# A merge and an output projection whose first inputs are loaded one stage earlier, and a last tile of a layer norm that another engine scales

## The reference, cut to what matters

```python
z = x @ w_in + b_in        # its last 3072 columns are mg, the pre-activations of three merge gates
# branch A: causal conv, RG-LRU scan, gelu gate        -> ya (1024 wide)
# branch B: stick-breaking attention                   -> yb (512 wide)
# branch C: mLSTM matrix memory in blocks, layer norm  -> yc (512 wide), and the new states c, n, m
mix = sigmoid(g_a) * (ya @ w_pa) + sigmoid(g_b) * (yb @ w_pb) + sigmoid(g_c) * (yc @ w_pc)
x1  = LN1(alpha * x + mix @ w_out)
y   = LN2(alpha * x1 + MoE(x1) + sigmoid(x1 @ Wg + bg) * (p @ Wp))     # top 4 of 32 experts
```

## Time and profile before

| | us |
|---|---|
| median of 3 runs | 2816.36 (2815.64 to 2816.7) |
| the profiled execution, its own time | 2818.67 |
| its span, first to last instruction | 2816.9 |
| TensorE busy in the span | 2557.3 (91%) |
| VectorE busy | 1580.7 (56%) |
| ScalarE busy | 1332.0 (47%) |
| GpSimd busy | 622.9 (22%) |
| merge, first to last matmul | 944.2 to 1445.4 |
| output projection, first matmul to end of the stage | 1452.4 to 1577.3 |

### The profile page before, as it was taken

The page is one execution under the profiler, slowest core; times in us unless marked ns, Lnnn a source line. Parts: engine busy times, 40 slices in busy tenths (PEclk is TensorE's granted clock), DMA queues, the critical chain, the costliest instruction groups (busy, mean ns, idle before and its releaser), DMA issues. The chain is left out here.

```text
span 2816.9 us, 40711 instructions
## 1 busy us (share of the span) xinstructions
PE 2557.3 (91%) x15168; PEld 2299.0 (82%) x15168; DVE 1580.7 (56%) x2533; ACT 1332.0 (47%) x2070; POOL 622.9 (22%) x494
## 2 busy tenths in 40 slices
PE   7998799999888799999989888599999999999990
PEld 6997687887567699999978567599999999998990
DVE  4665312118557545445444465577777777777774
ACT  4665311116432443334331222477777777777762
POOL 1000100004101011010114231143343343333433
PEclk9999989999999799999999899799999999999995
DMA  8221223202482755565543311688888898898864
GB/s 250 73 61 43 71 79 114 86 27 105 170 271 63 153 150 144 129 157 142 136 140 114 104 53 64 220 276 256 264 273 246 274 273 247 272 270 251 272 190 160
DMA packets 391375, 467.99 MB, mean 166 GB/s; under 512 B 21565, under 2 KB 314549, under 8 KB 391258
## 3 DMA queue, kind: packets, MB, share of 16 engines
q1 hardware_dynamic: 369160, 395.81, 45.9%
q0 software_dynamic: 17760, 60.34, 8.9%
q10 hardware_dynamic: 4338, 10.23, 0.9%
HBM read 397.62 MB, written 68.70 MB: 166 GB/s over the span
## 5 line engine op out<-in xcount | busy, mean ns | idle before, releaser
L3120 PE MATMUL banks<-slot_rowsT,expert_w_high 128*128 128x384 f32 x2048 | 603.7, 363 | 0.2 <-DVE slot_rowsT L3221 0.2
L3122 PE MATMUL banks<-slot_rowsT,expert_w_low 128*128 128x192 f32 x2048 | 515.2, 252 | 0.0
L3122 PEld LDWEIGHTS banks<-slot_rowsT,expert_w_low 128*128 128x128 f32 x2048 | 392.6, 192 | 1.3
L3120 PEld LDWEIGHTS banks<-slot_rowsT,expert_w_high 128*128 128x128 f32 x2048 | 385.8, 188 | 2.0 <-issue 0.6
L3156 ACT CAST expert_w_high<-expert_w 128x2048 fp32r<-128x2048 f32 x128 | 238.1, 1909 | 20.5 <-DMA expert_w<-in_exp_w 20.5
L3215 DVE TENSOR_TENSOR expert_w_low<-expert_w,expert_w_high 128x2048 fp32r<-128x2048 f32 x96 | 216.8, 2285 | 21.0 <-ACT expert_w_high L3156 21.0
L2068 PE MATMUL banks<-xT_chunk_high,w_gates_high 128*128 128x384 f32 x576 | 193.3, 336 | 15.7 <-DVE xT_chunk_low L2136 15.7
L3025 POOL TENSOR_TENSOR expert_w_low<-expert_w,expert_w_high 128x2048 fp32r<-128x2048 f32 x32 | 147.7, 4616 | 266.8 <-ACT expert_w_high L3156 266.8
L2069 PE MATMUL banks<-xT_chunk_low,w_gates_high 128*128 128x384 f32 x576 | 193.1, 335 | 0.0
L2070 PE MATMUL banks<-xT_chunk_high,w_gates_low 128*128 128x384 f32 x576 | 193.0, 335 | 0.0
L3281 DVE TENSOR_TENSOR expert_w_low<-expert_w,expert_w_high 128x1024 fp32r<-128x1024 f32 x128 | 157.2, 1228 | 54.5 <-ACT expert_w_high L3185 54.5
(11 more groups left out here) (498 smaller groups left out, 6122.8 us busy)
## 6 DMA issues: line engine op xcount, KB each, us to landing
expert_w<-in_exp_w SPq DMA_DIRECT2D x128, 1024.0 KB
expert_w<-in_exp_w SPq DMA_DIRECT2D x32, 2048.0 KB
w_gates<-in_w_in SPq DMA_DIRECT2D x72, 512.0 KB, 4.6
cached_k<-in_cache_sb_k SPq DMA_DIRECT2D x16, 1024.0 KB, 10.3
cached_v<-in_cache_sb_v SPq DMA_DIRECT2D x16, 1024.0 KB, 11.1
w_stream<-in_w_in SPq DMA_DIRECT2D x48, 256.0 KB, 4.4
w_proj<-in_w_pa SPq DMA_DIRECT2D x24, 512.0 KB, 5.1
w_stream<-in_w_in SPq DMA_DIRECT2D x16, 512.0 KB, 5.0
```

Source lines behind the costliest of these rows:

```text
L3120: nc.tensor.matmul(out[:, 0:2 * SLOTS], hi, xgT[:, par, k].rearrange("p a s -> p (a s)"), start=(k == 0), stop=(k == DT - 1), skip_group_c ...
L3122: last = nc.tensor.matmul(out[:, 0:SLOTS], lo, xgT[:, par, k, 0, :], start=False, stop=(k == DT - 1), skip_group_check=True)
```

## The change

- A new class `MixInputs` owns the merge's raw tiles `xa`, `wg`, `wp` and their DMA semaphores. It is made before `stage_mlstm`, and its `load_ahead` is called in that stage's SyncE stream behind `m.o_gate`: gate weights of unit 0, both halves of x's first chunk, projection weights of unit 0, then both weights of unit 1. `stage_mix` loads only from unit 2 on.
- In the merge, the casts and low parts of unit 0 stand in another order: gate weights, x, projection weights.
- A new class `OutInputs` owns the ring of `w_out` pieces and its semaphores. The ring has three places and not four. Its first three pieces are loaded at the end of the merge's SyncE stream; `stage_out` loads the other 13.
- The multiply and the add of the first norm's last row tile stand on VectorE behind its normalise, and no longer on GpSimd; those who read the tile wait for a new semaphore, `x1_last`.
- The new semaphores live in a second `stage_semaphores` of `early`, so there is one more clearing and barrier where `early` closes, between the routing and the experts.

```diff
@@ stage_mlstm, SyncE
             sp.dma_start(m.o_gate[:], g.mo_d.rearrange("i p n -> p i n")).then_inc(o_in, 16)
+            load_ahead(sp)
             sp.wait_ge(c_ready, 8)
@@ MixInputs
+    def load_ahead(self, sp):
+        self.load_gate_w(sp, 0, 1, 0)
+        self.load_x(sp, 0)
+        self.load_proj_w(sp, 0, 1, 0)
+        self.load_gate_w(sp, 1, 1, 1)
+        self.load_proj_w(sp, 1, 1, 1)
@@ OutInputs
+    WR = 3
+    def load(self, sp, n):
+        half, k = divmod(n, DT)
+        sp.dma_start(self.w[:, n % self.WR, :], self.source[:, k, half * 512:(half + 1) * 512]
+                     ).then_inc(self.w_in[n % self.WR], 16)
@@ stage_mix, SyncE (end)
+            for n in range(OutInputs.WR):
+                out_early.load(sp, n)
@@ stage_mix, ScalarE (VectorE the same with the low parts)
-            w_high_part(0)
+            gate_w_high_part(0)
             x_high_part(0)
+            proj_w_high_part(0)
@@ stage_out
-    R, WR = 3, 4
+    R, WR = 3, OutInputs.WR
@@ stage_out, SyncE
-            for n, (half, k) in enumerate(pieces):
-                if n >= WR:
-
-                    sp.wait_ge(w_split, n - WR + 1)
-                sp.dma_start(w[:, n % WR, :], wv[:, k, half * 512:(half + 1) * 512]).then_inc(w_in[n % WR], 16)
+            for n in range(WR, len(pieces)):
+
+                sp.wait_ge(w_split, n - WR + 1)
+                early.load(sp, n)
@@ stage_out, VectorE (end)
+            dve.wait_ge(norm_in, 32)
+            dve.wait_ge(hat_ready, NT)
+            nc.vector.tensor_tensor(x[:, s, :], x[:, s, :], norm[:, 0, :], ALU.mult).then_inc(last_scaled, 1)
+            dve.wait_ge(last_scaled, 1)
+            nc.vector.tensor_tensor(x[:, s, :], x[:, s, :], norm[:, 1, :], ALU.add).then_inc(x1_last, 1)
@@ stage_out, GpSimd
-            for i in range(NT):
+            for i in range(NT - 1):
@@ build_program
+                sem = early.enter_context(stage_semaphores(nc))
+                mix_early = MixInputs(nc, late, sem, g)
...
+                with ExitStack() as pieces:
+                    out_early = OutInputs(nc, pieces, sem, g)
+                    stage_mix(nc, g, xT, qT, ycT, mix_early, out_early)
+                    late.close()
+                    sem = early.enter_context(stage_semaphores(nc))
+                    route = RouteInputs(nc, early, sem, g)
+                    stage_out(nc, g, xT, xT, out_early, route.load_ahead)
```

More of the change, by code:

```diff
@@ L1972, in _, with __init__, sb, load_gate_w @@
                 nc.vector.tensor_tensor(hc[:, i, :], hc[:, i, :], m.o_gate[:, i, :], ALU.mult).then_inc(yc_ready, 1)
-def stage_mix(nc, g, mixT, yb, yc):
+class MixInputs:
+    def __init__(self, nc, ctx, sem, g):
+        def sb(name, shape):
+            return ctx.enter_context(nc.sbuf_tensor(name, shape, F32))
+        self.g = g
+        self.xa = sb("xT_then_yaT_chunk", [P, DT, CHUNK3])
+        self.wg, self.wp = sb("w_gates", [P, 2, DT, P]), sb("w_proj", [P, 2, DT, P])
+        self.x_in = [sem("x_x_in0"), sem("x_x_in1")]
+        self.wg_in = [sem(f"x_wg_in{i}") for i in range(2)]
+        self.wp_in = [sem(f"x_wp_in{i}") for i in range(2)]
+        self.src = ((g.w_pa, DT, 0), (g.w_pb, H, 0), (g.w_pc, H, H))
+    def load_gate_w(self, sp, n, r, m):
+        col = O_MG + r * D + m * P
+        sp.dma_start(self.wg[:, n % 2], self.g.w_in[0].rearrange("(k p) n -> p k n", p=P)[:, :, col:col + P]
+                     ).then_inc(self.wg_in[n % 2], 16)
+    def load_proj_w(self, sp, n, r, m):
+        w, kn, _ = self.src[r]
+        sp.dma_start(self.wp[:, n % 2, 0:kn, :], w[0].rearrange("(k p) n -> p k n", p=P)[:, :, m * P:(m + 1) * P]
+                     ).then_inc(self.wp_in[n % 2], 16)
+    def load_x(self, sp, c):
+        for half in range(2):
+            k = slice(4 * half, 4 * half + 4)
+            sp.dma_start(self.xa[:, k, :],
+                         self.g.xT_d.rearrange("k p t -> p k t")[:, k, c * CHUNK3:(c + 1) * CHUNK3]
+                         ).then_inc(self.x_in[half], 16)
+    def load_ahead(self, sp):
[4 more added lines that the diff above has]
+        self.load_proj_w(sp, 1, 1, 1)
+class OutInputs:
+    WR = 3
+    def __init__(self, nc, ctx, sem, g):
+        self.w = ctx.enter_context(nc.sbuf_tensor("w_out_piece", [P, self.WR, 512], F32, side="right"))
+        self.w_in = [sem(f"o_w_in{i}") for i in range(self.WR)]
+        self.source = g.w_out[0].rearrange("(k p) n -> p k n", p=P)
+    def load(self, sp, n):
+        half, k = divmod(n, DT)
+        sp.dma_start(self.w[:, n % self.WR, :], self.source[:, k, half * 512:(half + 1) * 512]
+                     ).then_inc(self.w_in[n % self.WR], 16)
+def stage_mix(nc, g, mixT, yb, yc, early, out_early):
     ORDER = [(r, m) for r in (1, 2, 0) for m in range(DT)]
@@ L1989, in stage_mix @@
         y_lo = sb("yT_chunk_low", [P, 2 * H, CHUNK3], F32R)
[L1990 to L1991 removed]
+        xa, wg, wp, x_in, wg_in, wp_in = early.xa, early.wg, early.wp, early.x_in, early.wg_in, early.wp_in
         wg_hi = sb("w_gates_high", [P, 2, DT, P], F32R)
         wg_lo = sb("w_gates_low", [P, 2, DT, P], F32R)
[L1994 removed]
         wp_hi = sb("w_proj_high", [P, 2, DT, P], F32R)
@@ L2015, in stage_mix @@
         block = ctx.enter_context(nc.Block())
-        SRC = ((g.w_pa, DT, 0), (g.w_pb, H, 0), (g.w_pc, H, H))
+        SRC = early.src
         Y_PARTS = {0: (0, yb, 0), 1: (H, yc, 0), DT: (0, xa, 0), 2 * DT: (H, xa, H)}
@@ L2024, in _ @@
         def _(sp):
[L2025 to L2031, removed]
             for n, (c, r, m) in enumerate(units):
@@ L2036, in _ @@
                     sp.wait_ge(wg_split, n - 1)
[L2037 to L2041, removed]
+                    early.load_gate_w(sp, n, r, m)
                     sp.wait_ge(wp_split, n - 1)
-                w, kn, _ = SRC[r]
-                sp.dma_start(wp[:, n % 2, 0:kn, :], w[0].rearrange("(k p) n -> p k n", p=P)[:, :, m * P:(m + 1) * P]
-                             ).then_inc(wp_in[n % 2], 16)
+                    early.load_proj_w(sp, n, r, m)
                 if n % U == 2 * DT + 2 and c + 1 < C:
                     sp.wait_ge(y_split, 4 * H * (c + 1))
-                    load_x(c + 1)
+                    early.load_x(sp, c + 1)
                 if n % U == 3:
@@ L2181, in _, with stage_out @@
                                        ALU.add).then_inc(add_ready, 1)
-def stage_out(nc, g, mixT, x1T, load_ahead):
-    R, WR = 3, 4
+def stage_out(nc, g, mixT, x1T, early, load_ahead):
+    R, WR = 3, OutInputs.WR
+    w, w_in = early.w, early.w_in
     pieces = [(half, k) for half in range(2) for k in range(DT)]
@@ L2202, in stage_out @@
         mv = sb("ln1_mean_var", [P, R, 2])
-        w_in = [sem(f"o_w_in{i}") for i in range(WR)]
         w_high = sem("o_w_high")
@@ L2251, in turn @@
             def turn(i):
-                pe.wait_ge(x1_ready, i + 1)
+                if i < NT - 1:
+                    pe.wait_ge(x1_ready, i + 1)
+                else:
+                    pe.wait_ge(x1_last, 1)
                 for half in range(2):
@@ L3471, in build_program @@
                     m.v_aug, m.o_gate = rb("ml_v", [P, NT, H, HD + 1]), rb("ml_o", [P, NT, 512])
-                    stage_mlstm(nc, g, m, ycT)
+                    stage_mlstm(nc, g, m, ycT, mix_early.load_ahead)
                 xT = early.enter_context(nc.sbuf_tensor("xT", [P, DT, T], F32, side="right"))
[L3474 to L3478, removed]
+                with ExitStack() as pieces:
[5 more added lines that the diff above has]
+                    stage_out(nc, g, xT, xT, out_early, route.load_ahead)
                 stage_route(nc, g, xT, route)
```

33 lines of the change are left out of this document (19 added, 14 removed).

## The result

| | before | changed |
|---|---|---|
| median, 15 runs each, us | 2814.46 (2809.12 to 2819.21) | 2804.51 (2798.04 to 2811.33) |
| ratio | | 0.9964, 95% interval 0.9955 to 0.9973 |
| the profiled execution, its own time | 2818.67 | 2800.07 |

The kernel became faster by 0.36%, 10.1 us of 2814.46 (7.6 to 12.7 by the interval). I had forecast a gain of 7.0 and a time of 2809.4, between 2806.3 and 2813.4. The sign and the order of size are right.

What follows compares the result with a forecast made beforehand. The prediction took TensorE's waits at stage starts and ends, with barriers that absorb nothing, to bound the kernel. Terms 9.0 - 3.8 + 2.3 - 0.5 = 7.0 us gave 2816.36 - 7.0 = 2809.4, range 2806.3 to 2813.4.

Steps and rivals of the forecast that it cites:

- What bounds the kernel, and where: Whole kernel: gains lie where TensorE stands still; stages end in barriers, so a shorter stage moves everything behind it.
- Part 1: Merge start: inputs loaded ahead let the first matmul start 9.0 us earlier, bounds 8.0 to 9.3.
- Part 2: Output projection, w_out ring of three: five rounds with landing time 3.2 us lose 3.8 us, bounds 1.3 to 6.8.
- The rival in which the ring is as fast as a lone load: Output projection's w_out ring: landing time 2.7, loss only 1.3 us, total gain 9.5, time 2806.9; chance 0.19.
- Part 3: End of output projection: last tile's two passes on VectorE instead of GpSimd gain 2.3 us, bounds 2.0 to 2.4.
- Part 4: Ahead of the experts: one more clearing and barrier costs 0.5 us, bounds 0.4 to 0.7.
- The clock: Rival: ring gaps put the second row tile at half clock, 2.0 us lost, 2811.4; chance 0.29, including landing above 3.6.
- The sum: Whole kernel: 9.0 - 3.8 + 2.3 - 0.5 = 7.0 us gained.
- The time: Whole kernel: median 2816.36 less 7.0 gives 2809.4 us, range 2806.3 to 2813.4.
- The chance of faster: Whole kernel: 0.64 that the measurement tells it faster, against same 0.33 and slower 0.03.

Runs made afterwards that it cites:

- again: The changed kernel profiled a second time with no edit; merge 507.7 us, output projection 128.3 us.
- e3: Changed kernel with the last tile's multiply and add back on GpSimd; output projection 130.6 us, merge 506.7 us.
- e4: Changed kernel with the old order of casts and low parts of unit 0 (gate weights, projection weights, x); merge 508.2 us.
- e6: Changed kernel with a second ring of eight places for the other 13 w_out pieces; median 2797.7 us, ratio 0.9934 to the kernel before.
- e2: Kernel before with a ring of three and not four w_out pieces, nothing loaded ahead; output projection 133.5 us, last low part 25.5 us behind the barrier.
- e5: Changed kernel with two places for w_out pieces, both loaded during the merge; output projection 137.9 us, last low part 33.0 us behind the barrier.

## Why the prediction was wrong, step by step

**What bounds the kernel, and where.** Right, as far as the scatter lets it be seen. The stages add up: nothing behind a barrier absorbed a gain or repaid one by more than the scatter of the later stages.

**Part 1, 9.0 us.** Right. The start of the merge is 12.1 - 3.0 = 9.1 us earlier, and the stage is shorter by 9.1 (mean of 516.0, 516.3, 515.9 against the mean of six profiles with the new start, 506.95). The chain was the one that I wrote down: TensorE starts 0.70 us behind the first low part of x, and the projection weights of unit 0, cast behind x, were not late. The matrix memory did not become longer, and its end was still set by the write of c_sample, for which SyncE waited 11.1 us. One number of the prediction is wrong and harmless: the early loads had 932.1 - 853.9 = 78 us before the first of them is read, not 58.

**Part 2, a loss of 3.8 us.** The mechanism is right, the size is not, and this is the step of the sum that failed: the landing time L of a piece in a ring of three was put at 3.2 us and measured 2.8. The formula (start at 3.05 behind the barrier, five rounds of L + 1.37) gives the measured 23.6 to 23.8 with L = 2.8. I reasoned from the refills of a ring of four, where they shared the DMA engines with two or three others (medians of 3.1 to 3.5 in three profiles), and took the first refill, 3.14, as the lower guide. In the ring of three the refills came 1.4 us apart on average, and a piece landed in 2.9 at the median in both profiles of the changed kernel, hardly slower than a lone one (2.7). Five rounds multiply an error in L by five: 0.4 too much in L is about 2 us too much in the sum. Against the profile that I worked from, the loss is 1.6; against the mean of three kernels with four late places, whose last low part came at 20.3 to 22.1, it is 2.4. The single profile hid that the old ring was itself uncertain by nearly 2 us. The rival in which the ring is as fast as a lone load (L = 2.7) came closest; I gave it 0.19. The estimate of 2.6 us for 256 KB, from the formula of the Trainium skill (DMA: Bandwidth & Descriptors, Anatomy of one DMA), was nearer than my choice too.

**Part 3, 2.3 us.** Right, 2.3 by the split above. **Part 4, 0.5 us.** Right: the barriers ahead of the experts stand 0.5 us apart, now three in place of two.

**The clock.** In none of the five profiles with three pieces loaded early (changed, again, e3, e4, e6) did the second row tile start at the half clock. In e2 it did, for 2 us, at a cost of 1.0. So the rival was real and half as dear as I priced it. What sets e2 apart is its late last piece: the wait of 1.37 us before it is longer than any that TensorE had in the first row tile of those five once the clock was up (0.98 at most). The length of one wait does not decide it, though: in e5 matmuls behind waits of 2.49 and 2.66 us still took 0.50 us, the time at the full clock. So what decides stays open, and why piece 15 was late in e2 does too.

**The sum.** Measured term by term it is 9.1 - 2.4 + 2.3 - 0.5 = 8.5 us with the mean of the old ring, or 9.4 - 1.6 + 2.3 - 0.5 = 9.6 with the two first profiles; the ratio of the runs says 10.1, and its interval, 7.6 to 12.7, holds both.

**The time.** Of the 4.9 us between 2809.4 and 2804.5, 1.9 are no matter of the change: the median of the three runs that I started from was 2816.36, that of 15 runs is 2814.46. Another 1.4 to 2.2 is the ring. The rest, 0.8 to 1.6, is inside the interval, and no run says where it comes from. Three runs within 1.1 us of each other looked like a kernel that repeats itself to 0.04%. It does not: the routing, the matrix memory, the attention over the cache and the recurrent branch each scatter by 3 to 7 us from execution to execution. My range was made of the bounds of the terms and held nothing for the starting point. The chance of faster, 0.64, was too low mainly by the same error in L.

Not settled: why the routing takes 189, 193 or 196 us. In the first profile of before, TensorE's longest wait there that no row explains is 7.8 us, in that of the changed kernel 3.3 (total, times, longest):

```profile
PE banks L2607 <- issue: 7.8, 1, 7.8
```

```profile
PE banks L2664 <- issue: 3.3, 1, 3.3
```

It comes while GpSimd sends the picks to memory, one after another. In the second profiles of both kernels, at 193.5 and 193.1, that wait is 3.2, so it can bear on the 196 only, and not on the step from 189 to 193. No run here was made for it.

## What to carry to other kernels

A ring that is refilled when its piece is used up runs in rounds: each round moves the last piece back by one landing time plus the work on a piece, so count rounds, not transfers. Loading the first pieces ahead saved 1.1 us here (their first low part ended 3.0 us behind the barrier in the changed kernel, 4.1 in e2), less than one round, and giving up a place of the ring for it cost more: 4.2 in e2, of which the late last piece is 0.9. The kernel of e6 got both: its early loads go to the memory that is free early, and a larger ring to the memory that becomes free later. And price a stage from several profiles, or from several runs that are not taken one behind the other, before you put a narrow range around a time.

## What the runs showed of the hardware

The landing time of a 256 KB piece rose with the number of places of the ring: median 2.8 us with two places (e5), 2.9 to 3.0 with three, 3.1 to 3.5 with four, 5.8 with eight (e6). The pieces still came faster, one every 2.1 us with two places, 1.4 with three, 1.1 to 1.2 with four, 0.7 with eight, where VectorE set the pace.

After the same start behind the same barrier, the clock of TensorE rose from 1.2 to 2.4 GHz some 3 us behind the first matmul in one execution of the changed kernel and some 2.4 us later in the next; over the six profiles with this start, the later the rise, the longer the merge, from 506.6 to 507.7.

In e5, with TensorE busy 14.30 of 25.30 us, the granted clock was 0.70 on average, a mix of both levels, and it was 1.2 GHz for part of the first 2 us of the steady work that followed (0.62), then 2.4. In e2 it was 2.4 GHz up to a wait of 1.37 us and 1.2 GHz behind it.
